# Squares added up on DVE before the row sums, row sums one tile later, and a weight split ahead of a conditioning step

## The reference, cut to what matters

```python
def rmsnorm(x, g):                                   # _rms(x) is the same without g
    return x * lax.rsqrt(jnp.mean(x * x, axis=-1, keepdims=True) + 1e-6) * g

# first_block, per layer
h = rmsnorm(x, g_mix_pre[l])
(a_q, a_k, a_v, ..., c_g) = jnp.split(h @ w_in[l], SPLIT_POINTS, axis=-1)
o_a = gated_deltanet(a_q, a_k, a_v, ...)   # conv, silu, then q and k divided by their norm in each head
o_b = dsa_attention(...)                   # scores of an indexer choose 128 keys per query
o_c = hgrn2(...)
x = x + rmsnorm(concatenate([o_a, o_b, o_c]) @ w_out[l], g_mix_post[l])
h = rmsnorm(x, g_ffn_pre[l])
x = x + rmsnorm(conv_geglu_ffn(h, ffn_w_up[l], ffn_conv[l], ffn_w_down[l]), g_ffn_post[l])

# second_block, per layer; mod = silu(c) @ w_ada[l] + b_ada[l]
x = x + 0.5 * gate(0) * _swiglu(norm_mod(x, 0), ...)
x = x + gate(1) * _mixer(norm_mod(x, 1), ...)
x = x + 0.5 * gate(2) * _swiglu(norm_mod(x, 2), ...)
```

## Time and profile before

| what | us |
|---|---|
| median of 3 runs (lowest, highest) | 4301.07 (4291.28, 4301.23) |
| the profiled execution, its time | 4292.86 |
| its span, first to last instruction | 4291.2 |
| PE busy | 3917.6 (91%) |
| DVE busy | 2150.6 (50%) |
| ACT busy | 1162.5 (27%) |
| PE share of the chain that ended last | 81% |
| mean granted TensorE clock | 0.953 |

### The profile page before, as it was taken

How to read it: one execution, slowest core, us unless ns; L and a number is a source line. 1 busy time by engine, 2 the same in 40 slices (tenths; PEclk the granted TensorE clock), 3 DMA queues, 4 the chain that set the end, 5 groups by cost and what they waited for, 6 DMA issues and landing times.

```text
span 4291.2 us, 52567 instructions
## 1 busy us (share of the span) xinstructions
PE 3917.6 (91%) x18982; PEld 3087.3 (72%) x18982; DVE 2150.6 (50%) x3500; ACT 1162.5 (27%) x1714; POOL 306.5 (7%) x503
## 2 busy tenths in 40 slices
PE   5899789997888888999799999999989999999998
PEld 4678647775667856778588777578868887856886
DVE  3657537752566636773555364355433334543332
ACT  2331313322323123332222233222222223332221
POOL 1020001110010000110011010011100001000000
PEclk8989889998998988999899999999999999999999
DMA  2210014542220013553355321145423333102332
GB/s 82 59 53 1 1 49 143 154 131 61 70 68 14 1 30 91 154 148 105 89 159 152 110 75 30 30 140 165 138 76 96 93 89 86 50 10 83 94 93 84
DMA packets 579514, 359.97 MB, mean 84 GB/s; under 512 B 20366, under 2 KB 559744, under 8 KB 579328
## 3 DMA queue, kind: packets, MB, share of 16 engines
q1 hardware_dynamic: 553920, 281.43, 23.6%
q0 software_dynamic: 25408, 76.11, 6.0%
HBM read 355.35 MB, written 2.10 MB: 83 GB/s over the span
## 4 chain that ended last, share of the span: by engine, by line
PE 81%; DVE 9%; issue 3%; ACT 3%; DVEq 2%; DMA 1%; POOLq 1%; SPq 0%; ACTq 0%; POOL 0%
PE ps L1214 15%; PE ps L1215 14%; PE ps L1216 14%; PE ps L1423 6%; PE ps L1426 6%; PE ps L1427 6%; PE ps L1263 5%; PE ps L1366 3%; PE ps L1547 3%; DMA wada<-in_w_ada 1%; DVEq L1915 1%; PE ps L1324 1%; PE ps L1346 1%; ACT wh L748 1%; PE ps L1709 1%
## 5 line engine op out<-in xcount | busy, mean ns | idle before, releaser
L1214 PE MATMUL ps<-hh,wh 128*128 128x512 f32 x2816 | 1129.0, 401 | 61.4 <-DVE wl L1912 35.1
L1215 PE MATMUL ps<-hl,wh 128*128 128x512 f32 x2816 | 1111.6, 395 | 0.0
L1216 PE MATMUL ps<-hh,wl 128*128 128x512 f32 x2816 | 1110.3, 394 | 0.0
L1912 DVE TENSOR_TENSOR wl<-wring,wh 128x1024 fp32r<-128x1024 f32 x476 | 581.1, 1222 | 833.1 <-ACT wh L748 826.3
L748 ACT ACTIVATE wh<-wring 128x1024 fp32r<-128x1024 f32 x496 | 522.1, 1055 | 1015.8 <-PE ps L1423 537.9
L1214 PEld LDWEIGHTS ps<-hh,wh 128*128 128x128 f32 x2816 | 539.3, 191 | 201.9 <-issue 65.8
L1216 PEld LDWEIGHTS ps<-hh,wl 128*128 128x128 f32 x2816 | 537.8, 191 | 115.1
L1215 PEld LDWEIGHTS ps<-hl,wh 128*128 128x128 f32 x2816 | 538.9, 191 | 110.7 <-issue 1.9
L1423 PE MATMUL ps<-ah,wh 128*128 128x512 f32 x1056 | 415.4, 393 | 2.6 <-DVE wl L1912 2.6
L1426 PE MATMUL ps<-al,wh 128*128 128x512 f32 x1056 | 411.8, 390 | 0.0
L1427 PE MATMUL ps<-ah,wl 128*128 128x512 f32 x1056 | 411.0, 389 | 0.0
(11 more groups left out here) (389 smaller groups left out, 4089.0 us busy)
## 6 DMA issues: line engine op xcount, KB each, us to landing
wring<-in_w_ffn_up SPq DMA_DIRECT2D x176, 512.0 KB, 4.9
wada<-in_w_ada POOLq DMA_DIRECT2D x384, 192.0 KB, 2.7
wring<-in_w_in SPq DMA_DIRECT2D x98, 512.0 KB, 4.9
wring<-in_ffn_w_up SPq DMA_DIRECT2D x88, 512.0 KB, 5.0
wring<-in_w_ffn_down SPq DMA_DIRECT2D x64, 512.0 KB, 4.0
wring<-in_w_out SPq DMA_DIRECT2D x32, 512.0 KB, 4.7
wring<-in_ffn_w_down SPq DMA_DIRECT2D x32, 512.0 KB, 4.0
wring<-in_w_ffn_down SPq DMA_DIRECT2D x16, 384.0 KB, 3.5
```

Of the source, the lines that this page charges most:

```text
L1214: pe.matmul(dst, w, h, start=first, stop=False)
L1215: pe.matmul(dst, w, hlo, start=False, stop=False)
L1216: return pe.matmul(dst, wlo, h, start=False, stop=last)
L1912: v.tensor_tensor(wl[:, w, :, :], wring[:, p, h, :, :], wh[:, w, :, :].bitcast(F32), ALU.subtract)\
```

## The change

1. **Summed norms.** For the norm behind the output projection and that behind the down projection, in both blocks, ACT still squares all 8 tiles, but DVE adds the squares of tiles 1 to 6 onto that of tile 0 (`sum_add`, one 128x512 addition each, placed in front of the eviction one tile later). PE then sums two buffers only, the total and tile 7's squares, at the end (`total_parts`). The parts inside the down projection are gone.
2. **Row sums of the delta rule** are taken behind tiles 9 to 16 instead of 8 to 15, and the first two indexer matmuls behind tile 0 of the 22 instead of in front of it.
3. **Split ahead of conditioning.** In `conv_first`, the last step of a half pair is conditioning and not the split.
4. **First tiles**: the second tile runs one k behind the first.

```diff
+def sum_slot(k):
+    return 0 if k == 0 else 1 + (k - 1) % 3
...
+            def sum_square(k, src):
+
+                if k == 0:
+                    s.wait_ge(sq_used.sem, n_sq[0])
+                if k >= 4:
+                    s.wait_ge(sq_used.sem, n_sq[0] + k - 3)
+                s.activation(sq[:, sum_slot(k), :], src, ACT.Square).then_inc(sq_ready.sem, 1)
+                if k == KD - 1:
+                    n_sq[0] += KD
...
                 def down_square(d):
                     y_ready.next(s)
-                    square(hT[:, d, :])
+                    sum_square(d, hT[:, d, :])
...
-                for k in range(KD):
-                    h_ready.next(pe)
+                for n in range(KD + 1):
                     for i in range(2):
+                        k = n - i
+                        if not 0 <= k < KD:
+                            continue
+                        if i == 0:
+                            h_ready.next(pe)
...
+            def total_parts(b):
+
+                pe.wait_ge(sq_used.sem, n_sq[0] + KD - 2)
+                if n_norm[0]:
+                    pe.wait_ge(std_done.sem, n_norm[0])
+                for j, slot in enumerate((0, sum_slot(KD - 1))):
+                    if j:
+                        sq_ready.next(pe, KD)
+                    for t in range(NT):
+                        m = pe.matmul(ps[0:NT, b, 0:P], stair[:, 31 - t:31 - t + NT], sq[:, slot, t * P:(t + 1) * P],
+                                      start=j == 0 and t == 0, stop=j == 1 and t == NT - 1)
+                    m.then_inc(sq_used.sem, 1)
+                n_sq[0] += KD
...
-                    if squares and n - 1 in DOWN_END:
-                        row_part(7, DOWN_END.index(n - 1), KD)
...
                 if squares:
-                    row_part(7, KD - 1, KD)
-                    row_cast(6)
+                    summed_norm()
...
-                index(0)
-                index(1)
                 for n in range(22):
                     tile(pool=n >= 14)
+                    if n == 0:
+                        index(0)
+                        index(1)
...
-                    if 8 <= n < 16:
-                        if n == 8:
+                    if 9 <= n < 17:
+                        if n == 9:
                             pe.wait_ge(ix_relu.sem, 12)
-                        stair_part(n - 8, 8)
+                        stair_part(n - 9, 8)
...
+            def sum_add(k):
+
+                v.wait_ge(sq_ready.sem, n_sq[0] + k + 1)
+                if k > 1:
+                    v.wait_ge(sq_used.sem, n_sq[0] + k - 1)
+                v.tensor_tensor(sq[:, 0, :], sq[:, 0, :], sq[:, sum_slot(k), :], ALU.add).then_inc(sq_used.sem, 1)
...
                             later(i, j, 1)
+                            split(whole=last and j == 1)
                             beside()
-                            split(whole=last and j == 1)
...
                     if n in DOWN_END:
+                        if squares and DOWN_END.index(n) >= 2:
+                            sum_add(DOWN_END.index(n) - 1)
                         down_done.next(v)
...
+                n_sq[0] += 22
                 for k in range(KD):
+                    if k >= 2:
+                        sum_add(k - 1)
                     b = filled()
                     v.tensor_copy(hT[:, k, :], ps[:, b, :])
```

More of the change, by code:

```diff
@@ L789, in norm, with wide_norm @@
                     .then_inc(std_done.sem, 1)
-            def wide_norm(srcs, before=None):
+            def sum_square(k, src):
[6 more added lines that the diff above has]
+                    n_sq[0] += KD
+            def wide_norm(srcs, before=None, summed=False):
                 for k, src in enumerate(srcs):
@@ L795, in wide_norm @@
                         before(k)
-                    square(src)
+                    if summed:
+                        sum_square(k, src)
+                    else:
+                        square(src)
                 s.wait_ge(sq_used.sem, n_sq[0])
@@ L1036, in y_square @@
                         split(after_out=True)
-                wide_norm([hT[:, k, :] for k in range(KD)], y_square)
+                wide_norm([hT[:, k, :] for k in range(KD)], y_square, True)
                 wide_norm([xT[:, k, :] for k in range(KD)], lambda k: x_ready.next(s))
@@ L1063, in down_square @@
                     x_ready.next(s)
-                    square(xT[:, d, :])
+                    sum_square(d, xT[:, d, :])
                 ffn(ACT.Silu, False, down_square)
@@ L1170, in x_square @@
                         split(after_out=True)
-                wide_norm([xT[:, k, :] for k in range(KD)], x_square)
+                wide_norm([xT[:, k, :] for k in range(KD)], x_square, True)
                 parts(lambda k: modP[:, 48 + k:49 + k])
@@ L1370, in row_part, with summed_norm @@
                 n_sq[0] += 1
+            def total_parts(b):
[10 more added lines that the diff above has]
+                n_sq[0] += KD
+            def summed_norm():
+                total_parts(7)
+                row_cast(6)
             def row_sums(b, n):
@@ L1727, in _ @@
                     out_pair(oT)
-                wide_norm()
+                summed_norm()
                 wide_norm()
@@ L1892, in begin @@
                 mm_done.seen[id(v)][1] = 1
-                n_mm[0] = n_split[0] = n_ada[0] = 0
+                n_mm[0] = n_split[0] = n_ada[0] = n_sq[0] = 0
                 half[:] = [0, 0]
@@ L1903, in _ @@
             n_ada = [0]
+            n_sq = [0]
             half = [0, 0]
@@ L1942, in factors @@
                 return ps[:, 1 + m % 3, :]
+            def sum_add(k):
[3 more added lines that the diff above has]
+                v.tensor_tensor(sq[:, 0, :], sq[:, 0, :], sq[:, sum_slot(k), :], ALU.add).then_inc(sq_used.sem, 1)
+                if k == KD - 2:
+                    n_sq[0] += KD
             def wide_root(splits=0):
@@ L2050, in conditioning, with ffn @@
                 i.then_inc(ada_step.sem, 1)
-            def ffn(dst, evicted, conv_first=False, ada=False):
+            def ffn(dst, evicted, conv_first=False, ada=False, squares=True):
                 beside = conditioning if ada else lambda: None
@@ L2777, in _ @@
                 v.drain().then_inc(mix_ready.sem, 1)
+                n_sq[0] += 12
                 for k in range(KD):
+                    if k >= 2:
+                        sum_add(k - 1)
                     b = filled()
@@ L2783, in _ @@
                 mod_norm(2, 2)
-                ffn(columns(1), lambda d, src: gated(src, 2, d), ada=l + 1 < DEPTH)
+                ffn(columns(1), lambda d, src: gated(src, 2, d), ada=l + 1 < DEPTH, squares=False)
                 end(l + 4)
```

## The result

The changed kernel takes 4202.4 us (median of 4 runs, 4192.5 to 4203.6) beside 4299.1 for the kernel before (4 runs, 4291.3 to 4301.2): ratio 0.977, 95% interval 0.975 to 0.979. That is 97 us gained where 134 were forecast, 37 us above the forecast and 2.4 above the upper end of the range.

The account below looks back on a forecast made before the run. PE's stream was taken as the bound, busy 3917.6 of 4291.2 us. Terms of 15.0 + 34.8 + 56.4 + 13.0 + 12.1 + 3.0 = 134.3 gave 4158 profiled, forecast as 4165; range 4145 to 4200.

Parts of the forecast that it names:

- E: Convolved feed-forward: split ahead of conditioning moves up 0.53 us a turn, 9 turns in each of two layers; 12.1 us gained.
- C: Projection behind the indexer: row sums one tile later end PE's waits for squares; 28.2 us a layer, 56.4 gained.
- Rivals 1 and 4: 1: weights late once row sums move, 4190, 9%; 4: something hidden holds the next tile as long, 4205, 3%.
- Rival 3: Projection: POOL's split doubled by DVE contention to 4.8 us, costing 27 us over 20 tiles; 4192, 3%.
- B: Down projections: summed norm removes seven row-sum parts between tiles; 8.7 us each, four times, 34.8 gained.
- A: Behind the output projection: summed norm brings the root 3.76 us earlier, in four places; 15.0 gained.
- F: Staggered first tiles: tile 0 ends one product earlier; an estimate of 3.0 us gained, bounds 0 and 5.
- D: First two indexer matmuls behind projection tile 0: tile 1 starts at 104.2; 6.5 us a layer, 13.0 gained.
- Rival 2: First block's denser projection: PE granted half clock, costing 280 us and making the kernel slower, 4445; 1%.

Follow-up runs that it names:

- four buffers: Changed kernel with four buffers for the conditioning weights instead of two: 4146.7 us with the split ahead of conditioning, 4159.1 us with it behind.
- the run with C alone: Kernel before with only the delta rule's row sums moved one projection tile on: 4223.8 us beside 4297.2, ratio 0.984.
- The kernel with the weights held back: Changed kernel, two buffers, with DVE announcing the free weight buffer some 2.1 us later: 4204.1 us, ratio 0.978 to the kernel before.
- the run without E: Changed kernel with the split put back behind the conditioning step in the convolved feed-forward: 4161.7 us, ratio 0.968 to the kernel before.

## Why the prediction was wrong

**E is the step that failed.** It said that the split moves up by 0.53, that the conditioning step is needed by PE only one tile later, and put the cost of moving that step at nothing. It followed only the result of the step. The step also frees a buffer and so makes POOL issue a load, and the prediction neither named that load nor asked what it would then stand behind. That load landed in 5.0 us where it had 3.05, and DVE waited 2.0 for it 18 times in the first layer's loop, 35.6 us. The price of the split itself was right (0.53 forecast, 0.63 a turn measured with four buffers, 12.1 and 12.4 in all). The load turned +12.1 into -41.6, which is 53.7 worse; the other parts gave 8.8 more than said. The two make the 45 us by which the profiled execution (4203.6) lies above its forecast (4292.9 less 134.3 is 4158.6; the prediction has 4158).

The rows that would have shown it stood in the trace of before: POOL's load at 669.02 and SP's two behind it, the median landing of 2.7 us, and the two taps with the wait of 1.39 ahead of them, which were all that stood between the split that lets the weights go and the step that lets the next load go.

**The range failed with it.** E's bounds were 5 and 18. Nothing excluded a loss, yet none was allowed for. The prediction's worst case of C and E together was 4188; with -10 in place of 5 for E it would have been 4203. (Its upper bound for E is added up wrongly too: 18 x 0.81 + 2.6 is 17.2 and not 18.)

**C** was right in its mechanism and nearly in its size: no waits, clock 1.00, 29.5 and 28.8 a layer for 28.2. Its 48.0 us for the stretch to tile 16 count eight row sums, while in the change the eighth stands behind tile 16; with seven the sum is 46.8, and 46.9 were measured (152.1 to 199.0) where it was 76.4 before (160.6 to 237.0). Rivals 1 and 4 are out. Rival 3 is too: POOL's splits took 2366 to 2412 ns in all 20 cases, beside whatever DVE did, and cost PE one wait of 0.3 us in the whole kernel.

**B** came to 9.9 and 9.8 in the first block for 8.7 (10.3 in the second layer, if E's last 0.5 is put where it belongs). **A** was right to 0.1 us in its chain (3.55 for 3.65). The stretch around it gained 6.7 and 9.0. In the first layer 3.9 of it are A's, and another 1.6 came in the norm that follows, which the prediction hadn't seen; what gives them was not tried. In the second block A and B together gave 21.0 for 24.9, F included: 7.4 and 7.2 at the down projections for 8.7, 2.2 each behind the mixer for 3.8. Why less stays open.

**D** has tile 1 at 102.21 where 104.2 was forecast. Most of the difference is not D's: the changed kernel is 1.8 us ahead before the place of D, and the run with C alone is 1.6 ahead at 74 us, before anything of it has run. From there on D gives 6.7 and, in the second layer, 7.2 for 6.5.

**Rival 2**, the clock, did not come in the form feared: the dense projection has 1.00. The clock did move the result in small steps, below.

## What to carry over

When an instruction is moved, follow not only who reads its result but also which buffer it frees and which load that lets go; then look at what stands ahead of that load in the DMA engines at its new time. A ring of two buffers that hardly ever made anyone wait may owe that to the work and the pauses that happen to stand between two issues; an edit that takes them away should be priced with the load's landing behind the largest transfer near it. Where a bound can't exclude a loss, let it go below zero.

## What the runs showed of the hardware

**Loads of different queues went one after the other, not side by side.** In the changed kernel POOL's 192 KB, issued 0.2 us behind SP's two loads of 512 KB, moved nothing in the window in which SP's queue moved 0.88 MB at 86% of the engines. It was so each time: 17 loads of the first layer's feed-forward were issued right behind 1 MB of weights and moved their first packet 3.2 to 3.6 us after their issue; those with no weights on the way did so after 1.2 to 1.4. The Trainium skill says (DMA: Bandwidth & Descriptors, Queues, rings and completion order) that each engine goes round the queues for which it has work, packet by packet; by that rule I would have expected the 192 KB to begin in turn with the weights. The measurement differs: the load began only when the 1 MB had all but passed and landed after 5.0 us instead of 2.7. The kernel with the weights held back shows the same for the load at 693.96, whose first packet moved 3.1 us after its issue. Why the engines did not take turns can't be read from these traces.

**Half clock comes in one execution and not in another, behind nearly the same activity.** The stretch in which PE multiplies the gated linear attention's output takes 17.2 us or 11.2. In two kernels that differ there in nothing, at the same place of the second layer (windows; the clock is the last but two; four buffers with the edit, then without):

```profile
1418.00:1438.00 20.00, 14.00 (x139) 12.21 (x139) 17.41 (x43) 15.04 (x31) 0.00 (x0) 0.86 0.00 1
1438.00:1456.00 18.00, 18.00 (x98) 11.84 (x98) 0.22 (x1) 1.60 (x4) 0.00 (x0) 0.57 0.00 1
```

```profile
1427.50:1447.50 20.00, 14.04 (x140) 12.51 (x139) 17.41 (x43) 15.05 (x31) 0.00 (x0) 0.85 0.00 1
1447.50:1459.00 11.50, 11.50 (x97) 7.86 (x96) 0.17 (x1) 1.14 (x3) 0.00 (x0) 1.00 0.00 1
```

In the 20 us ahead PE is busy for 14.0 us in both, and the clock was 0.86 and 0.85. Behind them one ran at about 1.2 GHz and the other at 2.4, a difference of 6 us. Both layers had the low level in the profile of before and of after, neither in the profile of the run without E; that would be 12 us of the 15 by which that execution (4147.1) lies below its kernel's median (4161.7), if the others had the low level. The five executions of this kernel stand in the order of their mean granted clock, from 4147.1 at 0.965 to 4168.0 at 0.959, so that most of the spread between runs of one kernel, here 21 us, is likely to be clock. What decides the level can't be read from these traces, and it stays open here.
